# Odd attention: GpSimd combines the two maps, VectorE copies the turned map of every odd unit

## The reference, cut to what matters

```
q, k, v = split(x @ w_in, 3)          # q, k get a rotary embedding; 8 heads x 2 maps x 64
s = einsum('bqhcd,bkhcd->bhcqk', qi, k) * scale
p = softmax(s)                        # over the 512 keys, for each of the two maps c
a = p[:, :, 0] - lam * p[:, :, 1]     # lam: one number worked out from lam_p
o = einsum('bhqk,bkhe->bqhe', a, v)   # v: 128 columns per head
o = rms_norm(o, subln_g) * (1 - lam_init)
mix = o @ w_out
```

## Time and profile before

| | |
|---|---|
| time, median of 3 runs | 2983.03 us (2982.72, 2983.03, 2989.16) |
| span of the profiled execution | 2987.6 us |
| busy: PE, DVE, ACT, POOL | 2913.4, 961.7, 744.5, 1642.4 us |
| granted TensorE clock | 9 tenths or more in nearly all of the 40 slices |

### The profile page before, as it was taken

One profiled execution on the slowest core, in us unless ns is written; L12 is line 12 of the kernel. 1 busy time (PEld: TensorE's weight loads), 2 busy tenths in 40 slices (PEclk: granted clock), 3 DMA queues, 4 the chain that ended last, 5 costly groups with the idle time before them and its releaser, 6 DMA issues.

```text
span 2987.6 us, 35633 instructions
## 1 busy us (share of the span) xinstructions
PE 2913.4 (98%) x14824; PEld 2434.3 (81%) x14824; DVE 961.7 (32%) x1447; ACT 744.5 (25%) x1492; POOL 1642.4 (55%) x1338
## 2 busy tenths in 40 slices
PE   8989999999999999999999999999999999999998
PEld 7777888888888768888888888788888887888887
DVE  3845404211025484141110333732110238521102
ACT  2236323101024373231100222542000233420001
POOL 4840472666657604726666467526666566166663
PEclk9999999999999999999999999999999998999999
DMA  4331331333223204213322332013222231132222
GB/s 141 99 127 57 114 126 57 99 99 99 99 85 120 71 15 141 99 57 113 99 94 92 105 99 95 5 39 113 92 97 99 99 106 57 35 113 94 99 99 85
DMA packets 184548, 271.21 MB, mean 91 GB/s; under 512 B 6708, under 2 KB 145972, under 8 KB 184388
## 3 DMA queue, kind: packets, MB, share of 16 engines
q1 hardware_dynamic: 174240, 243.28, 24.5%
q10 hardware_dynamic: 10148, 25.66, 2.6%
HBM read 266.79 MB, written 2.13 MB: 90 GB/s over the span
## 4 chain that ended last, share of the span: by engine, by line
PE 81%; DVE 8%; DMA 4%; POOL 3%; ACT 2%; issue 1%; ACTq 0%; DVEq 0%; POOLq 0%
PE PS L485 24%; PE PS L486 23%; PE PS L487 23%; POOL wlo L2395 3%; PE PS L877 3%; PE PS L574 2%; DVE a_qk L1303 2%; PE PS L863 1%; DVE nmx L1638 1%; PE PS L1031 1%; ACT whi L634 1%; DMA raw<-mem_wkv 1%; PE PS L1489 1%; DMA raw<-ffn_w 1%; DVE s_c L2283 0%
## 5 line engine op out<-in xcount | busy, mean ns | idle before, releaser
L2395 POOL TENSOR_TENSOR wlo<-raw,whi 128x512 fp32r<-128x512 f32 x881 | 1169.8, 1360 | 543.4 <-ACT whi L634 543.4
L485 PE MATMUL PS<-xT_hi,whi 128*128 128x512 f32 (+1 forms) x2304 | 848.0, 368 | 12.7 <-DVE xT_lo L594 6.4
L486 PE MATMUL PS<-xT_lo,whi 128*128 128x512 f32 (+1 forms) x2304 | 843.7, 366 | 0.0
L487 PE MATMUL PS<-xT_hi,wlo 128*128 128x512 f32 (+1 forms) x2304 | 843.5, 366 | 0.0
L2387 POOL TENSOR_SCALAR whi<-raw 128x1024 fp32r<-128x1024 f32 x384 | 416.6, 1103 | 666.0 <-DMA raw<-ffn_w 226.0
L485 PEld LDWEIGHTS PS<-xT_hi,whi 128*128 128x128 f32 x2304 | 435.9, 189 | 88.5 <-DVE xT_lo L594 8.7
L486 PEld LDWEIGHTS PS<-xT_lo,whi 128*128 128x128 f32 x2304 | 435.9, 189 | 70.4 <-issue 1.0
L487 PEld LDWEIGHTS PS<-xT_hi,wlo 128*128 128x128 f32 x2304 | 435.8, 189 | 70.3
L1073 DVE TENSOR_TENSOR htmp<-sil,PS 128x512 f32<-128x512 f32 x88 | 56.5, 683 | 803.4 <-ACT sil L1058 803.4
L485 PE MATMUL PS<-whi,h_hi 128*128 128x512 f32 x704 | 274.8, 390 | 0.8 <-POOL wlo L2395 0.8
L487 PE MATMUL PS<-whi,h_lo 128*128 128x512 f32 x704 | 274.0, 389 | 0.0
(11 more groups left out here) (384 smaller groups left out, 3142.8 us busy)
## 6 DMA issues: line engine op xcount, KB each, us to landing
raw<-ffn_w SPq DMA_DIRECT2D x66, 1024.0 KB, 5.1
raw<-ffn_w_gu SPq DMA_DIRECT2D x44, 1024.0 KB, 5.1
raw<-ffn_w_down SPq DMA_DIRECT2D x22, 1024.0 KB, 4.9
raw<-mem_wkv SPq DMA_DIRECT2D x16, 1024.0 KB, 5.3
raw<-even_w_in SPq DMA_DIRECT2D x14, 1024.0 KB, 5.1
raw<-ev_w_in SPq DMA_DIRECT2D x14, 1024.0 KB, 5.2
raw<-odd_w_in SPq DMA_DIRECT2D x12, 1024.0 KB, 5.2
raw<-od_w_in SPq DMA_DIRECT2D x10, 1024.0 KB, 5.1
```

What stands on the lines that cost most here:

```text
L485: pe.matmul(o, lhs[0], rhs[0], start=start, stop=False, skip_group_check=True)
L486: pe.matmul(o, lhs[0], rhs[1], start=False, stop=False, skip_group_check=True)
L487: return pe.matmul(o, lhs[1], rhs[0], start=False, stop=stop, skip_group_check=True)
L2395: m = pool.tensor_tensor(wlo[b][:, cs], raw[b][:, cs], whi[b][:, cs].bitcast(F32), ALU.subtract)
```

## The change

GpSimd takes the combination over in two instructions: it scales the second map in place with the column `ratio`, waits for that (`scaled`), and adds the first map into d_a. VectorE keeps reciprocal and short operation (`map_ratio`), with four columns for `ratio` instead of two. The roots of groups 0 to 5 come on GpSimd behind units 8, 12 to 28, the last two behind all units. The copy of the turned map of every odd unit is VectorE's, behind its maxima and ratio; TensorE waits for the semaphore of the engine that copies. The last groups' mean squares and stores on VectorE are no longer all due right after the last maxima (step 32) but at their own step or step 35 (`flush`). Where GpSimd's share stands in its queue (`pool_at`) is not changed. Other stages pass no `by_dve` and keep their copies on ScalarE.

```diff
@@ -822,10 +823,19 @@
             behind = 4
             together = 1
 
-            def __init__(self, n, nk, s_banks, pt_banks, o_banks, group, s_free, p, pt, last_of):
+            def __init__(self, n, nk, s_banks, pt_banks, o_banks, group, s_free, p, pt, last_of, by_dve=lambda u: False):
                 self.n, self.nk, self.s_banks, self.pt_banks, self.o_banks = n, nk, s_banks, pt_banks, o_banks
                 self.group, self.s_free, self.p, self.pt, self.last_of = group, s_free, p, pt, last_of
                 self.u0 = counts.get("units", 0)
+                self.by_dve = by_dve
+                of_dve = [u for u in range(n) if by_dve(u)]
+                first = {True: counts.get("turned_by_dve", 0), False: counts.get("turned_by_act", 0)}
+                self.turned_out = []
+                for u in range(n):
+                    first[by_dve(u)] += 1
+                    self.turned_out.append((pt_sb_dve if by_dve(u) else pt_sb, first[by_dve(u)]))
+                count("turned_by_dve", len(of_dve))
+                count("turned_by_act", n - len(of_dve))
                 self.g0 = counts.get("groups", 0)
                 self.groups = group(n - 1) + 1
                 count("units", n)
@@ -858,13 +868,13 @@
                     pe.wait_ge(*weights_ready(u))
                     if u >= 2:
 
-                        pe.wait_ge(pt_sb, A.u0 + u - 1)
+                        pe.wait_ge(*A.turned_out[u - 2])
                     for k in range(A.nk(u)):
                         m = pe.transpose(PS[:, A.ptb(u), 128 * k:128 * k + 128], A.p(u)[:, 128 * k:128 * k + 128], ident)
                     m.then_inc(pt_psum, 1)
                 if i > A.lag:
                     u = i - A.lag - 1
-                    pe.wait_ge(pt_sb, A.u0 + u + 1)
+                    pe.wait_ge(*A.turned_out[u])
                     g = A.group(u)
                     if g not in opened:
                         opened.add(g)
@@ -882,12 +892,13 @@
             for i in range(A.n + A.lag):
                 if i >= A.lag:
                     u = i - A.lag
-                    act.wait_ge(pt_psum, A.u0 + u + 1)
-                    if u >= 2:
-
-                        act.wait_ge(pv_done, A.u0 + u - 1)
-                    w = 128 * A.nk(u)
-                    act.activation(A.pt(u)[:, 0:w], PS[:, A.ptb(u), 0:w], ACT.Copy).then_inc(pt_sb, 1)
+                    if not A.by_dve(u):
+                        act.wait_ge(pt_psum, A.u0 + u + 1)
+                        if u >= 2:
+
+                            act.wait_ge(pv_done, A.u0 + u - 1)
+                        w = 128 * A.nk(u)
+                        act.activation(A.pt(u)[:, 0:w], PS[:, A.ptb(u), 0:w], ACT.Copy).then_inc(pt_sb, 1)
                     more(u)
                 if begun <= i < A.n:
                     exps(i)
@@ -896,18 +907,28 @@
 
             todo, to_prepare = [], []
             behind = A.behind
+            flush = A.n + (A.lag if any(A.by_dve(u) for u in range(A.n)) else 0)
             for i in range(A.n + behind + 1):
+                turned_u = i - A.lag
                 if i < A.n:
                     stats_(i)
+                if 0 <= turned_u < A.n and A.by_dve(turned_u):
+                    dve.wait_ge(pt_psum, A.u0 + turned_u + 1)
+                    if turned_u >= 2:
+
+                        dve.wait_ge(pv_done, A.u0 + turned_u - 1)
+                    w = 128 * A.nk(turned_u)
+                    dve.tensor_copy(A.pt(turned_u)[:, 0:w], PS[:, A.ptb(turned_u), 0:w]).then_inc(pt_sb_dve, 1)
+                if i < A.n:
                     if A.last_of(i):
                         todo.append((i, A.group(i)))
                         to_prepare.append((i, A.group(i)))
 
-                while prepare and to_prepare and (to_prepare[0][0] + behind - 1 <= i or i >= A.n):
+                while prepare and to_prepare and (to_prepare[0][0] + behind - 1 <= i or i >= flush):
                     u, g = to_prepare.pop(0)
                     dve.wait_ge(pv_done, A.u0 + u + 1)
                     prepare(g)
-                while todo and (todo[0][0] + behind <= i or i >= A.n):
+                while todo and (todo[0][0] + behind <= i or i >= flush):
                     u, g = todo.pop(0)
                     dve.wait_ge(pv_done, A.u0 + u + 1)
                     store(g, A.ob(u)).then_inc(o_out, 1)
@@ -1525,13 +1546,14 @@
 
         def stage_odd(st, jobs):
             A = Units(8 * NT, lambda u: 4, [0, 2], [4, 5], [6, 7], lambda u: u // 4, exp_done,
-                      lambda u: d_a[:, u % 3, :], lambda u: d_pt[:, u % 2, :], lambda u: u % 4 == 3)
+                      lambda u: d_a[:, u % 3, :], lambda u: d_pt[:, u % 2, :], lambda u: u % 4 == 3, lambda u: u % 2 == 1)
             A.behind = 7
             chunk = lambda c: slice(128 * c, 128 * c + 128)
             swapped, swap_read = S_("rope_swapped"), S_("rope_swap_read")
             rope_jobs = [j for j in jobs if j.name in "qk"]
-            lam_in, lam_exp, sq_in, sq_done, rms_in, rms_root = (S_(n) for n in (
-                "lam_sums", "lam_exp", "rms_sums", "rms_squares", "rms_in", "rms_root"))
+            lam_in, lam_exp, sq_in, sq_done, rms_in, rms_root, ratio_ready, scaled = (S_(n) for n in (
+                "lam_sums", "lam_exp", "rms_sums", "rms_squares", "rms_in", "rms_root", "map_ratio", "map_scaled"))
+            ratio_of = lambda u: scol[:, 24 + u % 4:25 + u % 4]
             gain = scol[:, 22:23]
             rms_cols = lambda g: [rec[:, o:o + 4] for o in (8 * (g % 2), 8 * (g % 2) + 4)]
 
@@ -1619,18 +1641,15 @@
                     return m
                 evacuations(dve, "dve", jobs, evac)
 
-                def combine(u):
+                def map_ratio(u):
                     dve.wait_ge(exp_done, A.u0 + u + 1)
-
-                    ratio = scol[:, 24 + u % 2:25 + u % 2]
-                    step(dve.reciprocal(ratio, rsum[:, 2 * u + 1:2 * u + 2]))
-                    step(dve.scalar_tensor_tensor(out=ratio, in0=ratio, scalar=scol[:, 21:22],
-                                                  in1=rsum[:, 2 * u:2 * u + 1], op0=ALU.mult, op1=ALU.mult))
-                    if u >= 3:
-
-                        dve.wait_ge(pt_psum, A.u0 + u - 2)
-                    dve.scalar_tensor_tensor(out=d_a[:, u % 3, :], in0=d_p[:, u % 3, 1, :], scalar=ratio,
-                                             in1=d_p[:, u % 3, 0, :], op0=ALU.mult, op1=ALU.add).then_inc(p_ready, 1)
+                    if u >= 4:
+
+                        dve.wait_ge(scaled, u - 3)
+                    step(dve.reciprocal(ratio_of(u), rsum[:, 2 * u + 1:2 * u + 2]))
+                    dve.scalar_tensor_tensor(out=ratio_of(u), in0=ratio_of(u), scalar=scol[:, 21:22],
+                                             in1=rsum[:, 2 * u:2 * u + 1], op0=ALU.mult, op1=ALU.mult)\
+                        .then_inc(ratio_ready, 1)
 
                 def stat(u):
                     dve.wait_ge(s_ready, A.u0 + u + 1)
@@ -1638,9 +1657,9 @@
                     dve.tensor_reduce(nmx[:, n:n + 2], PS[:, 2 * (u % 2):2 * (u % 2) + 2, :], AX_X, ALU.max, negate=True)\
                         .then_inc(stat_ready, 1)
                     if u >= 1:
-                        combine(u - 1)
+                        map_ratio(u - 1)
                     if u == A.n - 1:
-                        combine(u)
+                        map_ratio(u)
 
                 heads = lambda ap: ap.rearrange("p (h d) -> p h d", h=4)
 
@@ -1666,10 +1685,25 @@
                     dve_turn(dve, xT_hi, xT_lo, 0, KD, 2 * t, t, gain)
 
             def pool(pool):
-                for g in range(8):
+                def root(g):
                     pool.wait_ge(rms_in, g + 1)
                     ms, rstd_ = rms_cols(g)
                     pool.tensor_tensor(rstd_, ms, rec[:, 16:20], ALU.pow).then_inc(rms_root, 1)
+
+                for u in range(A.n):
+                    pool.wait_ge(exp_done, A.u0 + u + 1)
+                    pool.wait_ge(ratio_ready, u + 1)
+                    second = d_p[:, u % 3, 1, :]
+                    pool.tensor_scalar(second, second, ratio_of(u), None, ALU.mult).then_inc(scaled, 1)
+                    pool.wait_ge(scaled, u + 1)
+                    if u >= 3:
+
+                        pool.wait_ge(pt_psum, A.u0 + u - 2)
+                    pool.tensor_tensor(d_a[:, u % 3, :], second, d_p[:, u % 3, 0, :], ALU.add).then_inc(p_ready, 1)
+                    if u >= 8 and u % 4 == 0:
+                        root(u // 4 - 2)
+                root(6)
+                root(7)
 
             def pe(pe):
                 pe_split(pe, jobs, 1)
```

More of the change, by code:

```diff
@@ L305, in build @@
         pt_sb = sem("pt_sb")
+        pt_sb_dve = sem("pt_sb_dve")
         pv_done = sem("pv_done")
```

## The result

The changed kernel takes 3016.41 us (median of 4 runs, 3013.42 to 3019.3), the kernel before on the same chip 2983.99: ratio 1.0101, 95% interval 1.0084 to 1.0118. That is 32 us slower where 14.3 had been forecast, and 13 us above the end of the range, 3003. The profiled execution is the run of 3013.42, its span 3011.6.

What follows compares the result with a forecast made beforehand. TensorE, holding 81% of the chain, was taken to bound the kernel. The terms 12.1 + 1.6 - 3.2 + 2.9 + 0.9 = 14.3 us, against the median of 2983.03, gave 2997.3 us, range 2990.5 to 3003.

Steps and rivals of the forecast that it cites:

- The late start: Odd attention's start: GpSimd's share waits behind the third panel's cutting, so the first turning starts 12.1 us later.
- The clock's 1.6 us: Behind TensorE's idle start: half clock for 3.4 us of continuous work, a loss of 1.6 us.
- 3.2 us of hiccups: Units 4 to 8 of the odd attention: the old loop's delays there are gone, 3.2 us gained.
- the price of the scaling: GpSimd's scaling of 128x512 by a column: 0.66 us taken, bounds 0.66 and 1.28.
- costs over 1 us (then GpSimd alone binds, +20 or more): Sign of a wrong forecast: scaling with a column over 1 us makes GpSimd alone bind the loop, +20 or more.
- something else: Any other outcome, either way, including a scaling at 1.28 us (+25 in all); chance 0.05.
- The blocking step: Attention loop from unit 9: GpSimd and VectorE block each other, 10.9 us per four units, +2.9 (bounds -1.1 and +5.1).
- The walk: Four loop units followed through VectorE's and GpSimd's mutual waits: 10.8 to 11.3 us, over TensorE's 10.16.
- rival B: Late start alone, the loop staying at TensorE's 2.54 us a unit: +10.3, 2993.3 us; chance 0.20.
- The tail: From the last scores' end to the row turns: 9.0 us instead of 8.1, +0.9.
- The size of what could be gained: Odd attention loop: 3.3 us, with a 1.05 us wait 4.4 us, is all it could give back.
- not slower: Third panel not ahead of the first map, start costs nothing: 3.4 us faster or 1.5 slower; chance 0.05.

Runs made afterwards that it cites:

- two operations: Changed kernel with GpSimd's scaling given a second operation, times 1.0, same result; ratio 1.0025 (1.0014 to 1.0036) to the kernel before.
- both mends: Changed kernel with the two-operation scaling and GpSimd's share before the third panel's cutting; ratio 0.9993 to the kernel before, 0.9986 with copies also on ScalarE.
- broadcast product: Changed kernel with the scaling written as a product with the column spread over 512 elements; ratio 1.0050 (1.0035 to 1.0065) to the kernel before.
- Out of place: Changed kernel with the scaled map written to the sum's buffer instead of in place, still one operation; one run of 3016.86 us.

## Why the prediction was wrong

**Direction, place and start were right.** The late start was forecast as 12.1 us. Measured 13.1 (15.3 less 2.2), and 12.0 once the scaling is fast (14.2 less 2.2).

**The clock's 1.6 us were too small.** With the scaling mended, first to last turning takes 79.4 us with the idle start and 77.9 without, and the difference, 1.6, looks like the forecast. It is so by luck. All but 0.04 of it lies before S(5), and it has two parts. With two operations alone, T(0) and S(5):

```profile
1030.97 1.08 PE L873 MATMUL PS<-par,d_a 128*128 128x128 f32 x4 [12.24 <-POOL d_a L1702]
...
1036.74 1.16 PE L1714 MATMUL PS<-d_kT,d_qT 64*128 64x512 f32 x4
```
with both mends, S(4) and S(5), behind a T(0) at 1022.67:
```profile
1024.38 1.13 PE L1714 MATMUL PS<-d_kT,d_qT 64*128 64x512 f32 x4 [1.06 <-ACT d_p L1593]
...
1026.92 1.13 PE L1714 MATMUL PS<-d_kT,d_qT 64*128 64x512 f32 x4
```

From T(0) to S(5) it is 5.77 us with the idle start and 4.25 without; but the 4.25 hold 1.06 us of S(4)'s wait for exponentials, which the late start spares. So the low clock cost about 2.6 us there, since it lasted for 5.9 us of work and not for 3.4; the wait was in the forecast's 3.2 us of hiccups. In the changed kernel, where it lasted for 3.8 us, the cost was hidden behind GpSimd.

**The step that failed is the price of the scaling.** "Bounds are 0.66 and the addition's 1.28; I take 0.66, the nearer in form": it was 1.57, outside both bounds, and so the loop was not one in which blocking adds a little to TensorE's period, but GpSimd's alone. The row was near in shape and type but not in form: the earlier trace rows's instruction had two operations, the new one has one. With 1.57 a pair is 2.9 and four with a root 12.8, over TensorE's 10.16 and everything else. Mending it alone gives back 19.7 us of the 30.9 (115.8 against 96.1): 1.1 at the start, 17.8 between first and last turning, 0.8 behind. The bound from the nearest rows stopped at rows of other operations; this operation's own form had no row, and the prediction said so only for its column, which turned out to cost 0.07. Its own sign of being wrong came true ("costs over 1 us (then GpSimd alone binds, +20 or more)"), though not for the reason that it gave, the column; but it had a chance of 0.05 at most ("something else"), and the range ended below it.

**The blocking step failed too, by itself the smaller.** The walk gave 10.8 to 11.3 per four units. With a scaling of 0.69, which is what it assumed, four units take 10.16: rival B had the loop right for such a kernel. Against its +10.3 stand 11.2 measured in the stretch, the difference being mainly the clock. Two of the walk's assumptions are seen to fail in that run:

```profile
1060.00 0.69 POOL L1697 TENSOR_SCALAR d_p<-d_p,scol 128x512 f32<-128x512 f32 x1 [0.44 <-DVE scol L1650]
1060.34 0.36 DVE L1670 SCALAR_TENSOR_TENSOR rec<-rsum 128x4 f32<-128x4 f32 x1
...
1060.74 0.16 DVE L1672 SCALAR_TENSOR_TENSOR rec<-rec 128x4 f32<-128x4 f32 x1
1060.78 1.27 POOL L1702 TENSOR_TENSOR d_a<-d_p 128x512 f32<-128x512 f32 x1
...
1062.01 1.02 POOL L1691 TENSOR_TENSOR rec<-rec 128x4 f32<-128x4 f32 x1
...
1062.15 0.22 DVE L1650 SCALAR_TENSOR_TENSOR scol<-scol,rsum 128x1 f32<-128x1 f32 x1
```

VectorE's first short operation of the mean squares (L1670) waits only for the end of the scaling, 0.36 us in all, and the second (L1672, 0.16) comes in before the addition starts. And the root (L1691, 1062.01 to 1063.03) doesn't stop the next short operation (L1650 at 1062.15, 0.22). So GpSimd keeps up: from the scaling at 1052.87 to that at 1063.02, four units, it stands idle for 1.0 us in all. In the broadcast product's run, where GpSimd is just over TensorE's period, the blocking shows, as 0.5 us per four units.

**The tail** was forecast as 9.0 us from the last scores' end; 13.5 came, since three slow pairs stand one behind the other there and the clock fell once more. Out of place, with the same slow pairs and the clock at 1.00 to the end, it is 12.7, so the clock's part is about 0.8. With the mended scaling it is 1103.9 to 1112.85, 9.0.

**The size of what could be gained**, at most 4.4 us in the loop, is not contradicted: both mends give 2.4 to 2.5 in the stretch. The rival "not slower" named what decides: with the share early and a fast scaling the change is no longer slower (ratios 0.9993 and 0.9986).

The sum with the terms as measured, against before: start +13.1, first to last turning +16.8, from the last turning to the row turns 3.3 instead of 2.3, +1.0: 30.9. What stays open is why the one-operation form is slow on GpSimd; the runs only show that it isn't the column, nor the place, nor the output's type, and that a second operation takes it away.

## What to carry to other kernels

Price an added instruction by a row of its own form: engine, operation, number of arithmetic steps and operands. Where there is none, no neighbouring row is a bound, and the range has to say what happens if the price doubles, above all on an engine that is to become nearly full. Before work goes to an engine that runs a queue in fixed order, look at what stands ahead of it there: here a panel's cutting cost 13 us, and moving the share one place gave them back (12.9 in the stretch) without a wait elsewhere. Look into a difference that comes out as forecast, too: the 1.6 us of the clock were 2.6 less a wait that had gone. And compare what the loop can give back at most (4 us here) with what each mishap costs before moving the work at all.

## What the runs showed of the hardware

- On GpSimd a scaling of 128x512 float32 with one operation takes 1.57 us (1.49 with a constant), with a second operation, a multiplication by 1.0, 0.69. A product with a column spread over 512 elements takes 1.04, an addition of two maps 1.26.
- GpSimd's additions hold up VectorE's short operation with two inputs in SBUF until they end; its slow scalings do for their first 0.7 us alone. In the changed kernel:

```profile
1097.13 1.57 POOL L1697 TENSOR_SCALAR d_p<-d_p,scol 128x512 f32<-128x512 f32 x1 [0.19 <-DVE scol L1650]
...
1098.20 0.22 DVE L1650 SCALAR_TENSOR_TENSOR scol<-scol,rsum 128x1 f32<-128x1 f32 x1
...
1101.67 1.27 POOL L1702 TENSOR_TENSOR d_a<-d_p 128x512 f32<-128x512 f32 x1
...
1101.72 1.24 DVE L1670 SCALAR_TENSOR_TENSOR rec<-rsum 128x4 f32<-128x4 f32 x1
1102.91 1.57 POOL L1697 TENSOR_SCALAR d_p<-d_p,scol 128x512 f32<-128x512 f32 x1
...
1102.99 0.63 DVE L1672 SCALAR_TENSOR_TENSOR rec<-rec 128x4 f32<-128x4 f32 x1
```

Beside a scaling that runs to 1098.70, the short operation at 1098.20 takes 0.22. Beside an addition (1101.67 to 1102.94) the one at 1101.72 takes 1.24. Right behind a scaling's start, at 1102.99, one takes 0.63, and the scaling goes on for 0.9 us more. All seven that start so end 0.69 to 0.71 us behind the scaling's start, which is the length of the whole scaling with two operations (0.69); the earliest that starts later, 0.55 us in, takes its 0.22. The Trainium skill (SBUF — State Buffer, "Who interferes with whom") says that a VectorE instruction with two SBUF inputs contends with a GpSimd instruction that reads SBUF, and, of VectorE's two-port modes, that whoever issues first has the shared pair for the whole instruction. For the additions the trace agrees with "the whole instruction" (1.24 us); for the scaling of 1.57 us it doesn't, nor for the root (0.22 beside one of 1.02), and the measurement decides.
- In an idle of TensorE of 13.3 us the granted clock fell to 0.50 (1.2 in place of 2.4 GHz), and it was back at 1.00 after 3.8 us of work. In the kernel with two operations, behind an idle of 12.2 us, it took 5.9 us of work. At the end of the changed kernel's attention it fell again at about 1123.8, behind a wait of 2.1 us; in the kernel with two operations it stayed at 1.00 there, with waits of 0.3, 0.9 and 0.5 us.
